# Who adds the expert values of the later rows: TensorE and VectorE by halves, or VectorE alone outside the attentions

## The chip, the cores and the metric

The kernel runs on one core of one Trainium2 chip. The metric is the device time of one execution in microseconds, median over runs. All arithmetic is fp32 (float32r, in high and low parts, for the large weight products).

## The reference, cut to what matters

Two transformer blocks over 512 tokens of width 1024. The first ends in a layer of experts (`peer_ffn`): each token takes 128 experts of 16384 (8 heads, 16 each), and

```python
ue = jnp.take(expert_u, expert, axis=0)          # 128 rows of 1024 per token
ve = jnp.take(expert_v, expert, axis=0)          # 128 rows of 1024 per token
h = jax.nn.gelu(jnp.einsum('thkd,td->thk', ue, xc), approximate=False)
return jnp.einsum('thk,thkd->td', gate * h, ve)
```

The second block is a differential attention, a feed-forward layer (1024 to 4096 to 1024, squared relu), a latent attention and another feed-forward layer.

## The kernel before

**Rows.** The experts are worked off in 512 "rows". Row n belongs to token tile tt = n // 128 (128 tokens, one on each partition) and to the k-th chosen expert, k = n % 128. For a row, GpSimd issues one indirect DMA (line 1708) that brings for each of the 128 tokens 2048 numbers, u and v of its k-th expert, 1 MB in all. VectorE multiplies u by the token's x and sums (`dve_dot`, line 1826, 1024 columns, `accum_out`). ScalarE makes the gelu, the weight gate × gelu, and a diagonal matrix of the weights (`act_weight`, lines 1776, 1778, 1783). Then weight × v is added to the tile's sum in PSUM: up to row 255 TensorE does it alone, two products diag × v of 512 columns (line 1727). From row 256 on TensorE adds columns 0 to 511 into bank 6 and VectorE columns 512 to 1023 into bank 7, as one scalar_tensor_tensor (line 1808, with the weight as a scalar read from SBUF) that reads and writes PSUM. After k = 127 ScalarE copies the sums out (`act_join`, line 1792) and TensorE transposes them back (`pe_join`).

**Buffers.** From row 236 on the rows go round six buffers (`row_of`), so the gather of row n waits until row n - 6 has been added. `late` puts the adding of rows from 256 on one step later than the dot: in step s VectorE does the dot of row s + 1 and then the adding of row s - 1, and TensorE its product of row s - 1.

**What the later rows run beside.** Every engine has its own instruction list, in an order written out by hand. Rows 256 to 511 are interleaved with the second block's first 256 tokens (`tail(self.halves[0])`): `beside` takes one piece of the second block, adds its weight times RATE (1.1) to a due count, and lets as many row steps follow. So all engines have the row steps at the same places between the pieces, and each engine works strictly in order. A piece is one product group of 24 matmuls of 256 columns in the large layers (weight 1), or one block of an attention (weight 1.2; an attention has 16 blocks of scores and 19 such pieces). In the order of time: the join and the q, k and v products (27 pieces' weight), attention (22.8), its output layer with the norm of the heads (10), feed-forward (64), the second attention's projections (19.5), attention (22.8), its output layer (8), feed-forward (64, the rows end before it does). The second 256 tokens follow with no rows beside them.

**Weights of the second block** come in tiles of 512 KB (SyncE's queue, line 283). ScalarE makes the high part (`act_hi`, line 292), GpSimd the low part (`pool_lo`, line 298). GpSimd has both the low parts and the gathers in one list, so a gather that waits for its buffer holds up the low parts behind it. In a feed-forward layer VectorE scales a product (line 2503), ScalarE squares and rounds it (2487, 2491), VectorE makes the low part (2506); VectorE adds the layer's output to the residual (2530). The tail's products use PSUM banks 0 to 3.

Of the kernel before, what the change touches and what calls it, by code (L numbers as in the profile page):

```python
# [187 lines left out]
class Net:  # L188
    def __init__(self, nc, ctx, dram):
# [6 lines left out]
        self.spot, self.turn = {}, 0  # L196
        self.used, self.emptied = {}, {}
# [1210 lines left out]
    @staticmethod  # L1408
    def both_add(n):

        return n >= 256
# [275 lines left out]
    def pool_rows(self, e):  # L1687
        S = "peer_pool"
        lows = [k for k in self.keys if len(k) == 3]
        at = 0  # L1690
        for n in range(512):
            tt, k, r = n // 128, n % 128, self.row_of(n)
            before = self.row_before(n)
            while n >= FEW_ROWS + 12 and at < len(lows) and self.spot_before(lows[at]) <= self.spot.get(("row", before), 0):
                self.pool_lo(e, lows[at])
                at += 1
            if k == 0:
                e.wait_ge(*self.at("peer_dve", ("expert", tt)))
            if before is not None:
                e.wait_ge(*self.at("peer_pe", ("acc", before)))  # L1700
                if self.both_add(before):
                    e.wait_ge(*self.at("peer_dve", ("acc", before)))
            elif r == 0:
                e.wait_ge(*self.at("peer_pe", ("xn", 3, 1)))
            elif r == 6:
                e.wait_ge(*self.at("peer_pe", "mod20"))
            index = bass.IndirectOffsetOnAxis(ap=self.chosen[tt][:, k:k + 1], axis=0)
            e.indirect_dma_start(self.rows[r], None, self.d["peer_uv"], index).then_inc(*self.tick(f"row{r}", n, 16))  # L1708
        for key in lows[at:]:
            self.pool_lo(e, key)  # L1710
# [5 lines left out]
    def pe_rows(self, e):  # L1716
        S, D_, A_ = "peer_pe", "peer_dve", "peer_act"
        for step in range(-1, 512 + LAG):
            n = self.late(step)
            if n is not None:  # L1720
                tt, k = n // 128, n % 128
                b = 4 if tt == 0 else 6
                if k == 0 and tt >= 2:
                    e.wait_ge(*self.at(A_, ("sums", tt - 1)))
                e.wait_ge(*self.at(A_, ("diag", n)))
                for half in range(1 if self.both_add(n) else 2):
                    ins = e.matmul(self.ps[:, b + half, :], self.diag[n % 4],  # L1727
                                   self.rows[self.row_of(n)][:, 1024 + 512 * half:1536 + 512 * half], start=k == 0,
                                   stop=k == 127)
                ins.then_inc(*self.tick(S, ("acc", n)))  # L1730
                self.spot[("row", n)] = self.turn
# [18 lines left out]
    def act_rows(self, e):  # L1750
        S, D_, P_ = "peer_act", "peer_dve", "peer_pe"
        for n in range(-1, 512 + LAG):
# [5 lines left out]
            if n + 1 < 512:  # L1758
                self.act_weight(e, n + 1)
            if self.late(n) in (127, 255, 383, 511):  # L1760
# [6 lines left out]
            yield  # L1767

# [3 lines left out]
    def act_weight(self, e, n):  # L1772
# [7 lines left out]
        if n >= 4:  # L1780
            e.wait_ge(*self.at("peer_pe", ("acc", n - 4)))
# [3 lines left out]

    def act_join(self, e, tt):
        b = 4 if tt == 0 else 6
        e.wait_ge(*self.at("peer_pe", ("acc", 128 * tt + 127)))
# [5 lines left out]
    def dve_rows(self, e):  # L1794
        S, A_, P_ = "peer_dve", "peer_act", "peer_pe"
        for step in range(-1, 512 + LAG):
            if step + 1 < 512:
                self.dve_dot(e, step + 1)
            n = self.late(step)
            if n is not None and self.both_add(n):  # L1800
                v, w, acc = self.rows[self.row_of(n)][:, 1536:2048], self.weight[:, n % 128:n % 128 + 1], self.ps[:, 7, :]
                e.wait_ge(*self.at(A_, ("weight", n)))
                if n % 128 == 0:
# [11 lines left out]
    def dve_dot(self, e, n):  # L1815
# [6 lines left out]
        if self.both_add(n):  # L1822
# [235 lines left out]
    def attention(self, H, scores, softmaxed, turn, meet):  # L2058
        blocks = [(hh, qb) for hh in range(8) for qb in (2 * H.h, 2 * H.h + 1)]
        for n in range(len(blocks) + 3):  # L2060
# [8 lines left out]
            yield 1.2  # L2069

# [973 lines left out]
```

## Time and profile before

| | |
|---|---|
| median of 3 runs | 3439.2 us (3437.33 to 3441.46) |
| the profiled execution: its time | 3435.03 us |
| its span, first to last instruction | 3433.1 us |
| rows 256 to 511 beside the second block's first half | 1425 to 2580 us of the span |
| rows 0 to 255 | 760 to 1425 us |

Busy times are those of one profiled execution. The clock column is the share of TensorE's full speed that was granted (1.00 is 2.4 GHz, 0.50 is 1.2 GHz). The DMA column is the mean busy share of 16 DMA engines. "Idle before" is the time in which the engine stood still ahead of an instruction, with the instruction that let it go on.

### The profile page before, as it was taken

To read this page: it belongs to the slowest core of one execution; us is meant where nothing else is said; L and a number is where in the kernel's file an instruction comes from. 1 tells how busy PE (TensorE), PEld (TensorE's weight loads), DVE (VectorE), ACT (ScalarE), POOL (GpSimd) and SP (SyncE) were. 2 spreads that over 40 slices of the span, in tenths; PEclk is the share of its full clock that TensorE was granted. 3 is DMA by queue.
4 is the path that set the end of the run, shared out by engine and by line. 5 is a ranking of instruction groups with operands and counts; after the bars stand their busy time and mean duration, and the time that the engine had idled before them with its cause. 6 is when DMAs were issued, how large, how long until landed. Compare 5 with 4: busy or idle time off the path is not lost.

```text
span 3433.1 us, 43369 instructions
## 1 busy us (share of the span) xinstructions
PE 2812.6 (82%) x15438; PEld 2166.3 (63%) x15438; DVE 1986.8 (58%) x4260; ACT 1431.1 (42%) x3189; POOL 1659.1 (48%) x1014
## 2 busy tenths in 40 slices
PE   6987987778787777698688888688886979988897
PEld 4847986553333322385467766367776868977897
DVE  5775444457777767676665567675555453244422
ACT  2223222223333433457554445764443444344433
POOL 3812212363444433373276756266763426651674
PEclk8989998889999999797798988899987989999999
DMA  7210001329999998888598888888983314531453
GB/s 279 99 49 1 1 1 49 135 97 422 421 421 421 421 420 348 335 332 319 219 348 334 335 328 320 297 333 332 347 337 135 111 50 150 163 117 55 140 166 100
DMA packets 140518, 797.49 MB, mean 232 GB/s; under 512 B 15504, under 2 KB 18704, under 8 KB 67600
## 3 DMA queue, kind: packets, MB, share of 16 engines
q0 software_dynamic: 73728, 536.90, 38.9%
q1 hardware_dynamic: 65856, 253.36, 21.6%
q10 hardware_dynamic: 720, 4.46, 0.3%
q8 instruction: 124, 2.03, 0.2%
q14 instruction: 90, 0.74, 0.1%
HBM read 788.10 MB, written 6.55 MB: 231 GB/s over the span
## 4 chain that ended last, share of the span: by engine, by line
PE 39%; DMA 16%; POOL 12%; DVE 12%; issue 9%; ACT 6%; ACTq 0%; DVEq 0%; POOLq 0%; SPq 0%
PE ps L1727 7%; DMA raw<-in_peer_uv,un 6%; PE ps L2457 6%; POOL wls L298 6%; PE ps L870 6%; PE ps L1925 6%; DMA w<-in_peer_uv,un 5%; PE ps L328 4%; POOL wlw L298 4%; DMA un<-in_peer_uv,un 3%; PE ps L2435 2%; DVE scratch L1826 2%; POOL raw L1708 1%; DVE ps L1808 1%; PE ps L2122 1%
## 5 line engine op out<-in xcount | busy, mean ns | idle before, releaser
L298 POOL TENSOR_TENSOR wls<-raws,whs 128x1024 fp32r<-128x1024 f32 (+1 forms) x256 | 606.3, 2381 | 398.5 <-ACT whs L292 397.2
L1727 PE MATMUL ps<-raw,un 128*128 128x512 f32 x760 | 405.2, 650 | 134.1 <-ACT un L1783 131.8
L1708 POOL DMA_INDIRECT raw<-in_peer_uv,un x276 | 281.4, 1019 | 374.9 <-PE ps L1727 165.2
L1776 ACT ACTIVATE un<-un 128x1 f32<-128x1 f32 x512 | 103.6, 202 | 684.4 <-DVE scratch L1826 658.5
L292 ACT CAST whs<-raws 128x1024 fp32r<-128x1024 f32 (+1 forms) x256 | 260.8, 1036 | 198.7 <-PE ps L2457 85.4
L298 POOL TENSOR_TENSOR wlw<-raws,whw 128x1024 fp32r<-128x1024 f32 x112 | 265.7, 2389 | 110.8 <-ACT whw L292 110.4
L1727 PEld LDWEIGHTS ps<-raw,un 128*128 128x128 f32 x760 | 137.5, 203 | 278.1 <-ACT un L1783 199.3
L1925 PE MATMUL ps<-ts,whs 128*128 128x256 f32 x1424 | 298.1, 310 | 17.1 <-DVE ts L1994 9.6
L2457 PE MATMUL ps<-ts,whs 128*128 128x256 f32 x1216 | 261.1, 310 | 33.7 <-POOL wlw L298 29.9
L1727 PE MATMUL ps<-w,un 128*128 128x512 f32 x384 | 201.6, 670 | 88.7 <-ACT un L1783 88.7
L1925 PEld LDWEIGHTS ps<-ts,whs 128*128 128x128 f32 x1424 | 240.0, 204 | 46.9 <-issue 33.9
L1727 PE MATMUL ps<-un 128*128 128x512 f32 x392 | 217.3, 667 | 58.2 <-ACT un L1783 58.2
L1826 DVE SCALAR_TENSOR_TENSOR scratch<-raw,ps 128x1024 f32<-128x1024 f32 x172 | 209.0, 1215 | 75.3 <-DMA raw<-in_peer_uv,un 69.8
L1708 POOL DMA_INDIRECT un<-in_peer_uv,un x140 | 137.3, 981 | 214.4 <-DVE ps L1808 110.8
L2457 PEld LDWEIGHTS ps<-ts,whs 128*128 128x128 f32 x1216 | 203.9, 203 | 58.1 <-POOL wlw L298 32.3
L1783 ACT ACTIVATE un<-kept,un 128x128 f32<-128x128 f32 x512 | 205.7, 402 | 48.6 <-ACT un L1778 1.5
L2435 PE MATMUL ps<-ts,whw 128*128 128x256 f32 x960 | 202.7, 312 | 26.0 <-DVE ts L1994 22.9
L2435 PE MATMUL ps<-ts,whs 128*128 128x256 f32 x1088 | 220.5, 304 | 0.0
L1925 PE MATMUL ps<-ts,wls 128*128 128x256 f32 x712 | 208.9, 293 | 0.0
L1727 PEld LDWEIGHTS ps<-w,un 128*128 128x128 f32 x384 | 76.1, 210 | 208.0 <-ACT un L1783 136.6
L298 POOL TENSOR_TENSOR wl<-raw,wh 128x2048 fp32r<-128x2048 f32 x23 | 106.9, 4654 | 202.0 <-ACT wh L292 202.0
L2530 DVE TENSOR_TENSOR kept<-kept,ps 128x256 f32<-128x256 f32 x256 | 103.6, 418 | 164.4 <-PE ps L2457 163.4
(426 smaller groups left out, 7129.9 us busy)
## 6 DMA issues: line engine op xcount, KB each, us to landing
raws<-in_w_up SPq DMA_DIRECT2D x128, 512.0 KB
raws<-in_w_down SPq DMA_DIRECT2D x128, 512.0 KB
raws<-in_w_qk SPq DMA_DIRECT2D x32, 512.0 KB
scratch<-in_ada_w SPq DMA_DIRECT2D x13, 1024.0 KB, 14.4
raw<-in_w_in SPq DMA_DIRECT2D x11, 1024.0 KB, 5.8
raw<-in_ada_w SPq DMA_DIRECT2D x11, 1024.0 KB, 4.8
raw<-in_peer_w_q SPq DMA_DIRECT2D x8, 1024.0 KB, 7.0
raws<-in_w_v SPq DMA_DIRECT2D x16, 512.0 KB
```

What stands on the lines that cost most here:

```text
L292: e.copy(self.wh[h][:, 0:width], self.raw[slot][:, 0:width]).then_inc(*self.tick("hi", key))
L298: e.tensor_tensor(self.wl[h][:, 0:width], self.raw[slot][:, 0:width], self.wh[h][:, 0:width].bitcast(F32), ALU.subtract).then_inc(*self.ti ...
L328: ins = e.matmul(self.ps[:, b, :], l, r, start=k == 0 and i == 0, stop=k == nk - 1 and i == 2)
L870: ins = e.matmul(self.ps[:, b, 128 * q:128 * q + 128], l, r, start=n == 0, stop=n == len(terms) - 1)
L1708: e.indirect_dma_start(self.rows[r], None, self.d["peer_uv"], index).then_inc(*self.tick(f"row{r}", n, 16))
L1727: ins = e.matmul(self.ps[:, b + half, :], self.diag[n % 4], self.rows[self.row_of(n)][:, 1024 + 512 * half:1536 + 512 * half], start=k == ...
L1776: e.activation(self.gelus[:, c], self.dots[:, c], ACT.Gelu, bias=0.0, scale=1.0).then_inc(*self.tick(S))
L1783: e.activation(self.diag[n % 4], self.C("ident"), ACT.Identity, bias=0.0, scale=self.weight[:, c]).then_inc(*self.tick(S, ("diag", n)))
L1826: e.scalar_tensor_tensor(out=self.junk[n % 2 if n < 256 else 1], in0=self.rows[r][:, 0:1024], scalar=1.0, in1=xn, op0=ALU.mult, op1=ALU.mu ...
L1925: ins = e.matmul(o[:, 0:256], l, r, start=k == 0 and i == 0, stop=k == nk - 1 and i == 2)
L2435: ins = e.matmul(o[:, 0:256], l, r, start=k == 0 and n == 0, stop=k == 7 and n == 2)
L2457: ins = e.matmul(o[:, 0:256], l, r, start=n == 0, stop=n == 11)
```

## The change

Rows that are worked while an attention is being issued stay shared, as before. For all other rows from 256 on, VectorE adds all 1024 columns into banks 6 and 7 in one instruction; TensorE has no product and ScalarE makes no diagonal for them. VectorE's adding moves one step ahead for every row from 256 on: in step s it does the dot of row s + 1 and adds row s. TensorE's product of a shared row stays where it was. Where a shared stretch begins inside a token tile, TensorE can't continue VectorE's sum in bank 6, so ScalarE copies the bank to SBUF (`act_carry`) and TensorE starts its sum with ident × copy; where the stretch ends, VectorE waits once for TensorE's last product. A gather waits for TensorE only where row n - 6 was shared, and the copy at a tile's end (`act_join`) waits for VectorE's last row and for the last shared one.

```diff
+        self.shared_rows, self.attending = set(), False
...
-    @staticmethod
-    def both_add(n):
-        return n >= 256
+    def pe_adds(self, n):
+        return n < 256 or n in self.shared_rows
+
+    def pe_row_before(self, n):
+        return max((m for m in range(n - n % 128, n) if self.pe_adds(m)), default=None)
...
             if before is not None:
-                e.wait_ge(*self.at("peer_pe", ("acc", before)))
-                if self.both_add(before):
+                if self.pe_adds(before):
+                    e.wait_ge(*self.at("peer_pe", ("acc", before)))
+                if before >= 256:
                     e.wait_ge(*self.at("peer_dve", ("acc", before)))
...
+            if step >= 256 and self.attending:
+                self.shared_rows.add(step)
+            if n is not None and self.pe_adds(n):
...
+                first, last = k == 0 or not self.pe_adds(n - 1), k == 127 or not self.pe_adds(n + 1)
+                if first and k:
+                    e.wait_ge(*self.at(A_, ("carry", n)))
+                    e.matmul(self.ps[:, b, :], self.C("ident"), self.sums[tt % 2][:, 0:512], start=True, stop=False)
                 e.wait_ge(*self.at(A_, ("diag", n)))
-                for half in range(1 if self.both_add(n) else 2):
+                for half in range(2 if n < 256 else 1):
                     ins = e.matmul(self.ps[:, b + half, :], self.diag[n % 4],
-                                   self.rows[self.row_of(n)][:, 1024 + 512 * half:1536 + 512 * half], start=k == 0,
-                                   stop=k == 127)
+                                   self.rows[self.row_of(n)][:, 1024 + 512 * half:1536 + 512 * half],
+                                   start=first and k == 0, stop=last)
...
+            if n % 128 and self.pe_adds(n) and not self.pe_adds(n - 1):
+                self.act_carry(e, n)
...
-        if n >= 4:
-            e.wait_ge(*self.at("peer_pe", ("acc", n - 4)))
+        if not self.pe_adds(n):
+            return
+        user = max((m for m in range(n % 4, n, 4) if self.pe_adds(m)), default=None)
+        if user is not None:
+            e.wait_ge(*self.at("peer_pe", ("acc", user)))
...
+    def act_carry(self, e, n):
+        tt = n // 128
+        e.wait_ge(*self.at("peer_dve", ("acc", n - 1)))
+        if tt == 3:
+            e.wait_ge(*self.at("peer_pe", ("join", 1, 1)))
+        e.copy(self.sums[tt % 2][:, 0:512], self.ps[:, 6, :]).then_inc(*self.tick("peer_act", ("carry", n)))
...
-            n = self.late(step)
-            if n is not None and self.both_add(n):
-                v, w, acc = self.rows[self.row_of(n)][:, 1536:2048], self.weight[:, n % 128:n % 128 + 1], self.ps[:, 7, :]
+            n = step
+            if 256 <= n < 512:
+                w, row = self.weight[:, n % 128:n % 128 + 1], self.rows[self.row_of(n)]
+                v, acc = (row[:, 1536:2048], self.ps[:, 7, :]) if self.pe_adds(n) else (row[:, 1024:2048], self.sum_banks())
                 e.wait_ge(*self.at(A_, ("weight", n)))
+                pe = self.pe_row_before(n)
+                if pe is not None and not self.pe_adds(n):
+                    e.wait_ge(*self.at(P_, ("acc", pe)))
...
         blocks = [(hh, qb) for hh in range(8) for qb in (2 * H.h, 2 * H.h + 1)]
+        self.attending = True
         for n in range(len(blocks) + 3):
...
+        self.attending = False
```

## Rows read from the trace of the kernel before

**Rows 1.** The page: busy us, share of the span and instructions of each engine

```profile
PE 2812.6 (82%) x15438; PEld 2166.3 (63%) x15438; DVE 1986.8 (58%) x4260; ACT 1431.1 (42%) x3189; POOL 1659.1 (48%) x1014
```

**Rows 2.** Windows: length, busy of PE, PEld, DVE, ACT, POOL, clock, DMA share, GB/s

```profile
1425.00:1560.00 135.00, 114.82 (x707) 94.14 (x707) 93.86 (x198) 72.21 (x168) 84.40 (x52) 0.91 0.85 333
1560.00:1667.00 107.00, 85.75 (x273) 47.29 (x271) 80.38 (x229) 88.17 (x213) 26.29 (x27) 0.76 0.76 282
1667.00:1735.00 68.00, 46.97 (x260) 38.74 (x261) 40.34 (x86) 31.18 (x69) 33.75 (x21) 0.77 0.61 236
1735.00:2052.00 317.00, 270.14 (x1689) 226.69 (x1688) 188.89 (x369) 151.99 (x357) 207.32 (x132) 0.91 0.89 336
2052.00:2162.00 110.00, 83.92 (x424) 62.41 (x423) 84.21 (x158) 63.25 (x140) 65.83 (x44) 0.86 0.87 336
2162.00:2246.00 84.00, 56.72 (x196) 34.88 (x197) 53.89 (x137) 69.78 (x155) 20.00 (x22) 0.84 0.77 273
2246.00:2290.00 44.00, 35.65 (x239) 30.50 (x238) 33.80 (x56) 27.51 (x62) 35.85 (x21) 0.97 0.99 386
2290.00:2580.00 290.00, 249.46 (x1552) 208.68 (x1552) 165.80 (x320) 135.14 (x316) 190.36 (x117) 0.92 0.86 326
```

**Rows 3.** Instruction groups, 1425 to 2580 us: count | busy us, mean ns | idle before

```profile
L1826 DVE SCALAR_TENSOR_TENSOR scratch<-raw,ps 128x1024 f32<-128x1024 f32 x172 | 209.0, 1215 | 75.3 <-DMA raw<-in_peer_uv,un 69.8 <-ACT ps L1757 2.8 <-issue 2.6
L1727 PE MATMUL ps<-raw,un 128*128 128x512 f32 x345 | 201.2, 670 | 86.3 <-ACT un L1783 84.2 <-ACT un L1792 2.1
...
L1808 DVE SCALAR_TENSOR_TENSOR ps<-raw,un,ps 128x512 f32<-128x512 f32 x170 | 127.6, 751 | 0.0
...
L1727 PE MATMUL ps<-un 128*128 128x512 f32 x176 | 108.8, 706 | 28.8 <-ACT un L1783 28.8
...
L1783 ACT ACTIVATE un<-kept,un 128x128 f32<-128x128 f32 x258 | 103.7, 402 | 24.1 <-ACT un L1778 0.4
...
L1826 DVE SCALAR_TENSOR_TENSOR scratch<-un,ps 128x1024 f32<-128x1024 f32 x84 | 102.0, 1215 | 38.5 <-DMA un<-in_peer_uv,un 36.6 <-ACT un L1783 1.9
...
L1808 DVE SCALAR_TENSOR_TENSOR ps<-un,ps 128x512 f32<-128x512 f32 x84 | 63.1, 751 | 0.0
...
L2506 DVE TENSOR_TENSOR ts<-ps,ts 128x256 fp32r<-128x256 f32 x64 | 27.2, 425 | 131.2 <-ACT ts L2491 130.3 <-ACT ps L2487 0.8
...
L1994 DVE SCALAR_TENSOR_TENSOR ts<-kept,ts 128x256 fp32r<-128x256 f32 x32 | 15.5, 485 | 0.3 <-ACT ts L1966 0.3
```

**Rows 4.** The windows view of line 1727 alone, first feed-forward stretch

```profile
1735.00:2052.00 317.00, 81.65 (x142) 23.39 (x142) 0.91 0.89 336
```

**Rows 5.** Waits, 1735 to 2052 us: who waited for whom, us in total, times, longest

```profile
DVE ts L2506 <- ACT ts L2491: 65.5, 31, 5.6
POOL raw L1708 <- DVE ps L1808: 42.8, 20, 3.8
...
PE ps L1727 <- ACT un L1783: 35.8, 14, 7.5
POOL un L1708 <- DVE ps L1808: 24.4, 9, 5.6
DVE scratch L1826 <- DMA raw<-in_peer_uv,un: 20.1, 16, 2.7
...
DVE scratch L1826 <- DMA un<-in_peer_uv,un: 17.5, 12, 3.5
...
DVE ps L2503 <- PE ps L2435: 9.6, 10, 2.4
```

**Rows 6.** Timeline of VectorE: start, us, instruction, idle before it

```profile
1811.83 0.42 DVE L2506 TENSOR_TENSOR ts<-ps,ts 128x256 fp32r<-128x256 f32 x1 [0.84 <-ACT ts L2491]
```

**Rows 7.** Windows: TensorE after an idle gap; the second half without rows

```profile
1804.30:1809.10 4.80, 4.78 (x16) 3.75 (x17) 2.23 (x4) 3.25 (x9) 3.68 (x2) 0.50 0.76 239
...
2900.00:3000.00 100.00, 92.27 (x726) 91.57 (x726) 24.82 (x61) 42.55 (x64) 75.50 (x32) 0.95 0.53 163
```

**Rows 8.** Instruction groups of the whole run: a ScalarE copy of 512 columns

```profile
L1601 ACT COPY scratch<-ps 128x512 f32<-128x512 f32 x16 | 9.3, 587 | 39.2 <-PE ps L1573 21.6 <-DVE scratch L1675 15.5 <-PE ps L1727 2.0
```

More of the change, by code:

```diff
@@ L1719, in pe_rows @@
             n = self.late(step)
-            if n is not None:
+            if step >= 256 and self.attending:
+                self.shared_rows.add(step)
+            if n is not None and self.pe_adds(n):
                 tt, k = n // 128, n % 128
@@ L1724, in pe_rows @@
                     e.wait_ge(*self.at(A_, ("sums", tt - 1)))
+                first, last = k == 0 or not self.pe_adds(n - 1), k == 127 or not self.pe_adds(n + 1)
+                if first and k:
+                    e.wait_ge(*self.at(A_, ("carry", n)))
+                    e.matmul(self.ps[:, b, :], self.C("ident"), self.sums[tt % 2][:, 0:512], start=True, stop=False)
                 e.wait_ge(*self.at(A_, ("diag", n)))
-                for half in range(1 if self.both_add(n) else 2):
+                for half in range(2 if n < 256 else 1):
                     ins = e.matmul(self.ps[:, b + half, :], self.diag[n % 4],
-                                   self.rows[self.row_of(n)][:, 1024 + 512 * half:1536 + 512 * half], start=k == 0,
-                                   stop=k == 127)
+                                   self.rows[self.row_of(n)][:, 1024 + 512 * half:1536 + 512 * half],
+                                   start=first and k == 0, stop=last)
                 ins.then_inc(*self.tick(S, ("acc", n)))
+            if n is not None:
                 self.spot[("row", n)] = self.turn
@@ L1767, in act_rows, with sum_banks @@
             yield
+    def sum_banks(self):
+        return self.ps[:, 6:8, :].rearrange("p b n -> p (b n)")
     def xn_bank(self):
@@ L1784, in act_weight @@
                      scale=self.weight[:, c]).then_inc(*self.tick(S, ("diag", n)))
+    def act_carry(self, e, n):
[4 more added lines that the diff above has]
+        e.copy(self.sums[tt % 2][:, 0:512], self.ps[:, 6, :]).then_inc(*self.tick("peer_act", ("carry", n)))
     def act_join(self, e, tt):
         b = 4 if tt == 0 else 6
-        e.wait_ge(*self.at("peer_pe", ("acc", 128 * tt + 127)))
+        last = self.pe_row_before(128 * tt + 127) if tt >= 2 and not self.pe_adds(128 * tt + 127) else 128 * tt + 127
+        if last is not None:
+            e.wait_ge(*self.at("peer_pe", ("acc", last)))
         if tt >= 2:
@@ L1821, in dve_dot @@
         xn = self.XN[:, n // 128, :]
-        if self.both_add(n):
+        if n >= 256:
             e.wait_ge(*self.at("peer_act", ("xn", n // 128)))
```

## The prediction

> **What bounds the kernel now.** I read the page first: TensorE is busy 82% of the span and VectorE 58% [rows 1]. That average hides stages with different limits, so the next view is the windows of the stage that the change touches, 1425 to 2580 us, cut where the second block goes from one layer to the next [rows 2]. In it VectorE is busy 741 of 1155 us. In the two feed-forward stretches (317 and 290 us) TensorE is busy 85 and 86%, and the DMA engines 89 and 86%, since every row brings 1 MB and every piece of the second block a 512 KB weight tile.
>
> For one piece of weight 1 in a feed-forward layer, the first has 64 pieces in 317 us: 4.95 us per piece, with 1.1 rows in it. What does each engine need?
> - TensorE: in the second half, without rows, 726 matmuls take 100 us, so 24 take 3.31 us [rows 7]. The row products take 81.65 us for 71 rows, 1.15 us a row [rows 4]. Together 3.31 + 1.1 × 1.15 = 4.57 us, 92% of 4.95.
> - DMA: 0.89 × 4.95 = 4.41 us.
> - VectorE: 188.9 / 64 = 2.95 us, and half a wait of 0.84 us, the shortest that it has between lines 2503 and 2506 while ScalarE squares and rounds [rows 6]: 3.37 us.
>
> So two limits stand close together, TensorE just above DMA, and the in-order lists lose the rest. The waits of that stretch show how [rows 5]: TensorE stands 35.8 us for a row's diagonal, GpSimd 42.8 + 24.4 us for VectorE to have added the row whose buffer the next gather wants, and VectorE 65.5 us for ScalarE but only 9.6 us for TensorE's product.
>
> **The change part by part.** Each attention has pieces worth 22.8, so 22.8 × 1.1 = 25 rows; two attentions make 50 shared rows, and 206 of the 256 move.
> - *TensorE's products go*: 206 × 1.15 = 237 us of TensorE, out of the busiest engine. A feed-forward piece then needs 3.31 us of it. ScalarE loses 206 diagonals of 402 ns [rows 3], 83 us, and their wait for TensorE's product of row n - 4.
> - *VectorE's adding grows* from 512 to 1024 columns. No row shows this shape. A scalar_tensor_tensor with a scalar from memory takes 485 ns for 256 columns (line 1994) and 751 for 512 (line 1808), 266 ns for 256 columns more; so 751 + 532 = 1283 ns. The lower bound is the 1024-column dot that reads PSUM, 1215 ns (+464); the upper one is two of the old addings, 1502 (+751) [rows 3]. I take +532, as its rows are of the same kind: 206 × 0.532 = 110 us (96 to 155). A piece then needs 3.37 + 1.1 × 0.532 = 3.96 us of VectorE. Nothing hides this on VectorE itself, which works in order; it is covered only where VectorE would otherwise stand idle, 414 us in this stage, of which 106 us are waits for rows' data [rows 3].
> - *The adding moves a step ahead.* It now waits for the weight of a row whose dot was finished one dot earlier; the dot in between takes 1.2 us and ScalarE's gelu and weight are short, so I cost this at nothing. That cover is gone where ScalarE is stuck behind a weight tile that has not landed. Behind a waiting adding stand the next piece's scaling or residual, and TensorE waits for those. On the other side the buffer comes free one step (some 4.5 us) sooner: row n was added after the dot of row n + 2 and is now added after that of n + 1. Before, three rows beyond the one in work could be in flight, now four. GpSimd's 67 us of waits are what this shortens. Its list issues the same gathers and low parts in the same order.
> - *A gather no longer waits for TensorE* outside the attentions; TensorE can run ahead of the rows by its four free banks, so the 35.8 us go from it. In the attentions a gather waits for TensorE's product, which is still a step late, so little changes there.
> - *Two carries*: a copy of 512 columns, nearest 587 ns [rows 8], and one product more, 1.15 us, twice: 3.5 us if nothing covers it. The wait at the end of a shared stretch comes once each and I cost it at nothing, as TensorE's product is due in the same step; if TensorE lags, it is one piece.
>
> DMA's bytes stay. A feed-forward piece after the change needs 4.41 us of DMA, 3.96 of VectorE, 3.31 of TensorE. The floor moves from 4.57 to 4.41 only: that is why 237 us of TensorE's work can't come back as 237 us. How close the stretch comes to its floor is a choice: it is at 92% of its tightest engine now, and one stretch (2246 to 2290) shows DMA at 0.99 [rows 2]. I take a DMA share of 0.93, and let VectorE be busy at most 85% (the rows show up to 77%; the waits for ScalarE inside a piece leave no more):
> - 1425 to 1560: DMA 135 × 0.85 / 0.93 = 123; VectorE (93.9 + 24 × 0.532) / 0.85 = 125.5. New length 125.5, **-9.5**.
> - 1735 to 2052: 317 × 0.89 / 0.93 = 303, **-14** (VectorE 226.7, 75%).
> - 2290 to 2580: 290 × 0.86 / 0.93 = 268, **-22** (VectorE 165.8 + 66 × 0.532 = 200.9, 75%).
> - 2052 to 2162: VectorE (84.2 + 25 × 0.532) / 0.85 = 115; there the chain through norms and small pieces sets the time. **0**.
> - 2246 to 2290: DMA is full; VectorE (33.8 + 11 × 0.532) / 0.85 = 46.6, **+2.6**.
> - 1667 to 1735, where the norm of the heads leaves every engine waiting: **0**. The attentions: 0, with the carries **+3.5**.
>
> The sum is -39 us. From the profiled execution's 3435.0 us (its span of 3433.1 and 1.9 around it) that is 3396; that execution is 4.2 us under the median of the runs, so against the median it is 3439.2 - 39 = **3400 us**.
>
> **The clock.** TensorE's granted clock was 0.50 (1.2 GHz) from 1804.3 to 1809.1, after 7.5 us of waiting for a diagonal, and 0.91 over the first feed-forward stretch [rows 2, 5, 7]. The Trainium skill, "TensorE: Matmul & The Clock Gate" (HAM oscillation), says that an engine whose short bursts are parted by waits for data starts each burst cold; it speaks against making TensorE idler. By rows, a piece all at half clock would take 3.31 × 0.95 / 0.5 = 6.3 us instead of 4.95, +1.34 × 124 pieces = +166 us, 3605 us. TensorE decides only below a mean clock of 3.31 × 0.95 / 4.7 = 0.67, and the idlest stretches show 0.76 and 0.77 [rows 2]. By that rule, this case so far agrees only in part, and I give it 0.02.
>
> **The rivals.**
> - *The forecast*, 3375 to 3425: both feed-forward stretches move toward DMA's floor. Chance 0.45.
> - *DMA gets full* because a fourth row in flight keeps it fed: the stretches of 135, 317, 290 and 110 us shrink by their free DMA share (0.15, 0.11, 0.14, 0.13), 20 + 35 + 41 + 14 = 110 us, 3329 us. For it: GpSimd's 67 us of waits for buffers [rows 5]. Against it: VectorE would be at 80 to 100% in them. 3325 to 3375, chance 0.18.
> - *VectorE takes the place of TensorE and it comes out even*: in the first feed-forward stretch VectorE has 317 - 189 = 128 us idle. If only its waits for rows, 20.1 + 17.5, go, and those for ScalarE stay, the new length is 226.7 + 90.5 = 317 us. For it: VectorE hardly waits for TensorE. Against it: ScalarE is late partly because its diagonals wait for TensorE. Within 7 us of 3439: 0.14. Between this and the forecast, 3425 to 3432: 0.06.
> - *Slower*: VectorE's adding, now bound to the weight of the step before, waits for a ScalarE that stands behind a weight tile, so that VectorE keeps half of its row waits too. The 110 us are then paid and 53 come back: +57, 3496 us; it decides from where VectorE wins back less than 110 of its 414 idle us. For it: VectorE's largest wait is already for ScalarE. Chance 0.15.
> - If the change moved fewer rows than 206 (more of them counted as inside an attention), all terms shrink alike; the count of the new shape will tell. It gets no chance of its own.
>
> **How the numbers follow.** The time is the likeliest case's, 3400 us, its own range 3375 to 3425. The range for 8 in 10 leaves out the slow cases (0.17) and the bottom of the full DMA: 3335 to 3444. About 0.2%, 7 us, is what a measurement can tell from no change. Faster: 0.45 + 0.18 + 0.06 = 0.69; same 0.14; slower 0.15 + 0.02 = 0.17.
>
> **What the changed profile would show.** Right: some 206 instructions of VectorE with 1024 columns into PSUM at about 1.28 us, two copies by the carry; TensorE's busy time down by some 240 us; in the feed-forward stretches a DMA share of 0.93 or more, VectorE at 75%, GpSimd's waits for VectorE well under 67 us, and VectorE waiting more for ScalarE or DMA than for anything else. Wrong: a DMA share that stays at 0.89 with VectorE over 80% (the even case), VectorE waiting for the weight at its adding (the slower one), or a granted clock under 0.7. A price near 1.5 us for the new adding would cost 45 us of VectorE more and lead to the even case.

## The result, and the profile after

| | before | after |
|---|---|---|
| median | 3438.3 us (3435.5 to 3441.5, 4 runs) | 3465.8 us (3459.7 to 3468.9, 4 runs) |
| ratio, 95% interval | | 1.0083 [1.0070, 1.0096] |
| the profiled execution: its time / span | 3435.0 / 3433.1 us | 3465.0 / 3463.2 us |
| mean granted clock | 0.903 | 0.879 |

The change made the kernel 27.5 us slower, where 39 us faster was forecast. The page after, as in [rows 1]:

```profile
PE 2679.2 (77%) x15030; PEld 2139.4 (62%) x15030; DVE 2114.7 (61%) x4260; ACT 1348.8 (39%) x2985; POOL 1660.9 (48%) x1014
```

TensorE has 408 matmuls fewer in the records. Each product of a row is there as two, so these are 412 for 206 rows, less four for the two carries. Its busy time fell by only 133 us. VectorE gained 128 us with the same number of instructions.

The windows view, cut at the same events of the second block as [rows 2] (the first cut is at 1428 us, where both kernels are still level):

```profile
1428.00:1581.00 153.00, 98.50 (x641) 91.76 (x640) 130.68 (x190) 55.71 (x129) 75.03 (x48) 0.83 0.71 271
...
1750.00:2080.00 330.00, 230.07 (x1556) 221.84 (x1555) 229.97 (x376) 131.09 (x298) 219.69 (x138) 0.82 0.88 336
...
2312.00:2610.00 298.00, 207.24 (x1433) 200.25 (x1433) 206.44 (x333) 115.11 (x263) 197.91 (x122) 0.85 0.86 331
```

The same first stretch of the kernel before:

```profile
1428.00:1558.00 130.00, 110.54 (x694) 92.28 (x694) 91.18 (x193) 69.44 (x159) 81.86 (x50) 0.91 0.84 330
```

It took 130 us with VectorE busy for 91.18 of them. Now it takes 153, and VectorE is busy 130.68 us in it with three instructions fewer. That is 22 to 23 us lost in the stretch that the forecast had get 9.5 us shorter. The 17 + 8 larger addings of that stretch add 13 us to VectorE; something else adds 26, net. In the feed-forward stretches the DMA share did not rise (0.88 and 0.86, before 0.89 and 0.86), and they are 12 and 9 us longer over their whole lengths (318 to 330, 317 to 326). By the time of the second feed-forward layer's end the kernel after is 32 us behind; the remainder of the program takes 834 us in it and 836 in the kernel before.

The groups view of 1428 to 2629 us for the lines that answer to [rows 3]:

```profile
L1861 DVE SCALAR_TENSOR_TENSOR scratch<-raw,ps 128x1024 f32<-128x1024 f32 x172 | 208.8, 1214 | 54.4 <-DMA raw<-in_peer_uv,un 52.3 <-ACT ps L1770 2.1
L1843 DVE SCALAR_TENSOR_TENSOR ps<-raw,un,ps 128x1024 f32<-128x1024 f32 x137 | 175.9, 1284 | 7.3 <-ACT un L1796 7.3
...
L1843 DVE SCALAR_TENSOR_TENSOR ps<-un,ps 128x1024 f32<-128x1024 f32 x67 | 86.0, 1284 | 0.0
...
L2543 DVE TENSOR_TENSOR ts<-ps,ts 128x256 fp32r<-128x256 f32 x64 | 27.2, 425 | 101.7 <-ACT ts L2528 101.7
...
L1843 DVE SCALAR_TENSOR_TENSOR ps<-raw,un,ps 128x512 f32<-128x512 f32 x33 | 24.8, 752 | 2.3 <-ACT un L1796 2.3
...
L2179 DVE TENSOR_TENSOR q<-q,tmp 128x256 f32<-128x256 f32 x8 | 18.8, 2346 | 0.3
L2179 DVE TENSOR_TENSOR k<-k,tmp 128x256 f32<-128x256 f32 x8 | 18.7, 2342 | 0.3
```

The new adding is there 204 times, with two first rows of a tile in another form, 206 in all, at 1284 ns; the shared rows are 33 + 17 = 50. All waits of VectorE for the weight at its adding together are 7.3 + 2.3 + 1.1 us. The last two rows are the find. Line 2179 is the last instruction of the rotary step, `x = x + tmp` on 256 columns; it belongs to the second block, and the change does not touch it. In the kernel before, the same sixteen instructions, in the same view of 1428 to 1560 us:

```profile
L2142 DVE TENSOR_TENSOR k<-k,tmp 128x256 f32<-128x256 f32 x8 | 3.4, 426 | 0.3
L2142 DVE TENSOR_TENSOR q<-q,tmp 128x256 f32<-128x256 f32 x8 | 3.4, 425 | 0.3
```

37.5 us instead of 6.8: 31 us of VectorE. (Of its other instructions, the dots above all, some 4 us less fall into the window, hence the 26 net.) Fourteen of the sixteen take 2.57 to 2.64 us; the first and the last take 0.42. The timelines of VectorE and then GpSimd in the kernel after (start, us, instruction, idle before it) show what the instruction does in that time:

```profile
1504.78 1.28 DVE L1843 SCALAR_TENSOR_TENSOR ps<-un,ps 128x1024 f32<-128x1024 f32 x1
1505.98 0.41 DVE L2176 TENSOR_TENSOR tmp<-ps,rsin 128x256 f32<-128x256 f32 x1
1506.31 0.41 DVE L2177 TENSOR_TENSOR q<-q,rc 128x256 f32<-128x256 f32 x1
1506.76 2.63 DVE L2179 TENSOR_TENSOR q<-q,tmp 128x256 f32<-128x256 f32 x1
1509.31 1.21 DVE L1861 SCALAR_TENSOR_TENSOR scratch<-raw,ps 128x1024 f32<-128x1024 f32 x1
...
1510.45 1.28 DVE L1843 SCALAR_TENSOR_TENSOR ps<-un,ps 128x1024 f32<-128x1024 f32 x1
```

```profile
1506.71 2.40 POOL L299 TENSOR_TENSOR wls<-raws,whs 128x1024 fp32r<-128x1024 f32 x1 [1.77 <-ACT whs L293]
1509.25 0.96 POOL L1714 DMA_INDIRECT un<-in_peer_uv,un  x1
```

The sum starts 0.05 us after GpSimd's low part of a weight tile (line 299) and ends 0.28 us after it, at 1509.39. The profile books this as busy time, so no view of waits names it. The kernel before, VectorE and GpSimd:

```profile
1501.59 0.42 DVE L2139 TENSOR_TENSOR tmp<-ps,rsin 128x256 f32<-128x256 f32 x1 [1.14 <-PE ps L2134]
1501.93 0.42 DVE L2140 TENSOR_TENSOR k<-k,rc 128x256 f32<-128x256 f32 x1
1502.38 0.43 DVE L2142 TENSOR_TENSOR k<-k,tmp 128x256 f32<-128x256 f32 x1
1502.72 1.21 DVE L1826 SCALAR_TENSOR_TENSOR scratch<-raw,ps 128x1024 f32<-128x1024 f32 x1
```

```profile
1502.55 2.52 POOL L298 TENSOR_TENSOR wls<-raws,whs 128x1024 fp32r<-128x1024 f32 x1 [0.38 <-ACT whs L292]
```

Here the sum starts 0.17 us ahead of the low part and is done in 0.43 us; it is the low part that takes 2.52 us for 2.40. What sets the order is visible in the chains. After the change both instructions hang on the same event, the end of a dot (1504.86). On VectorE the adding (1.28 us) and two rotary instructions follow it; on ScalarE gelu, weight, a copy and the high part do, and the low part waits for that. Both chains take 1.85 to 1.9 us, so the two meet again in the next period, 5.67 us later. Before, VectorE's adding was 0.53 us shorter, its period was 4.17 us, and the two engines met only after a wait of 1.14 us for TensorE's product and with another phase. That the longer adding shifts the sums into the low parts is read from these chains; x2 and x3 below test it.

The Trainium skill, "SBUF — State Buffer" (the section "SBUF: two separate sides"), has the rule for it: VectorE and GpSimd share one pair of ports as an exclusive lock, and an instruction of VectorE with two inputs in SBUF waits for all of a GpSimd instruction that reads SBUF if that one started first. The rows above agree: `q` and `tmp` both lie in SBUF, the low part reads two tiles of SBUF, the sum that started 0.05 us after it was held and the one that started 0.17 us ahead of it was not, and the addings, whose second large input is the bank, keep their 1284 ns. Closer than 0.1 us the recorded starts do not follow the rule: see x14.

### The profile page after: what moved, and what is told of

Same layout as the page of the kernel before. It is cut to its first block, busy times and chain, and to the rows that moved or that the text cites. A ratio compares the mean times of both kernels' runs of the same rounds, so it can differ in the third digit from the quotient of the medians.

```text
span 3463.2 us, 41943 instructions
## 1 busy us (share of the span) xinstructions
PE 2679.2 (77%) x15030; PEld 2139.4 (62%) x15030; DVE 2114.7 (61%) x4260; ACT 1348.8 (39%) x2985; POOL 1660.9 (48%) x1014
## 4 chain that ended last, share of the span: by engine, by line
PE 35%; DMA 17%; DVE 17%; POOL 11%; issue 8%; ACT 7%; DVEq 0%; ACTq 0%; POOLq 0%; SPq 0%
DMA raw<-in_peer_uv,un 6%; PE ps L2494 6%; POOL wls L299 6%; PE ps L871 6%; DMA w<-in_peer_uv,un 5%; PE ps L1739 5%; PE ps L329 4%; PE ps L1960 4%; DVE scratch L1861 4%; POOL wlw L299 3%; DVE ps L1843 3%; DMA un<-in_peer_uv,un 3%; PE ps L2472 2%; DMA raws<-in_w_down 1%; ACT whs L293 1%
## 5 line engine op out<-in xcount | busy, mean ns | idle before, releaser
L2494 PE MATMUL ps<-ts,whs 128*128 128x256 f32 x1216 | 269.7, 318 | 123.9 <-POOL wlw L299 66.9
L1960 PE MATMUL ps<-ts,whs 128*128 128x256 f32 x1424 | 294.4, 308 | 24.5 <-DVE ts L2029 14.1
L2494 PEld LDWEIGHTS ps<-ts,whs 128*128 128x128 f32 x1216 | 222.1, 224 | 132.0 <-POOL wlw L299 71.8
L1739 PE MATMUL ps<-raw,un 128*128 128x512 f32 x482 | 250.9, 656 | 55.1 <-ACT un L1804 55.1
L1960 PEld LDWEIGHTS ps<-ts,whs 128*128 128x128 f32 x1424 | 246.3, 210 | 32.9 <-issue 16.2
L1861 DVE SCALAR_TENSOR_TENSOR scratch<-raw,ps 128x1024 f32<-128x1024 f32 x172 | 208.8, 1214 | 54.4 <-DMA raw<-in_peer_uv,un 52.3
L2494 PE MATMUL ps<-ts,whw 128*128 128x256 f32 x832 | 183.3, 314 | 71.9 <-POOL wls L299 33.2
L2472 PE MATMUL ps<-ts,whw 128*128 128x256 f32 x960 | 193.7, 303 | 47.6 <-DVE ts L2029 41.0
L1739 PEld LDWEIGHTS ps<-raw,un 128*128 128x128 f32 x482 | 92.8, 207 | 188.4 <-ACT un L1804 107.8
L1843 DVE SCALAR_TENSOR_TENSOR ps<-raw,un,ps 128x1024 f32<-128x1024 f32 (+1 forms) x170 | 200.7, 1180 | 9.6 <-ACT un L1796 9.6
L2472 PE MATMUL ps<-ts,whs 128*128 128x256 f32 x1088 | 197.8, 284 | 4.6 <-DVE kept L2567 3.2
```

What stands on the lines that cost most here:

```text
L1739: ins = e.matmul(self.ps[:, b + half, :], self.diag[n % 4], self.rows[self.row_of(n)][:, 1024 + 512 * half:1536 + 512 * half], start=first ...
L1843: e.scalar_tensor_tensor(out=acc, in0=v, scalar=w, in1=acc, op0=ALU.mult, op1=ALU.add).then_inc(*self.tick(S, ("acc", n)))
L1861: e.scalar_tensor_tensor(out=self.junk[n % 2 if n < 256 else 1], in0=self.rows[r][:, 0:1024], scalar=1.0, in1=xn, op0=ALU.mult, op1=ALU.mu ...
L1960: ins = e.matmul(o[:, 0:256], l, r, start=k == 0 and i == 0, stop=k == nk - 1 and i == 2)
L2472: ins = e.matmul(o[:, 0:256], l, r, start=k == 0 and n == 0, stop=k == 7 and n == 2)
L2494: ins = e.matmul(o[:, 0:256], l, r, start=n == 0, stop=n == 11)
```

## Experiments

Three theories stood at the start. *Held*: the rotary sums, held by GpSimd's instructions, cost the 28 us. *Larger adding*: VectorE's 110 us more cost it by themselves, held sums or not. *Step ahead*: the adding's earlier place costs it. The expectations call them theories A, B and C. Two more came later, on what sets the pace of the feed-forward layers: D, the transfers, and E, VectorE's in-order list. The medians of the kernel before in the three groups of runs are 3436.7, 3436.0 and 3435.5 us; each ratio is to the kernel before in its own group, so differences of medians across groups carry up to 3 us of drift. The ratios are not the quotients of the medians either: for x1 the two differ by 3 us.

**x1_rope_psum**: the kernel after, with the rotary product left in its PSUM bank, so that the sum has only one input in SBUF. The bank is thus given back only after the sum.

```diff
-        e.tensor_tensor(tmp, self.bh((P_, "rope", key)), rsin, ALU.mult)...
+        r = self.bh((P_, "rope", key))
+        e.tensor_tensor(r, r, rsin, ALU.mult)...
...
-        e.tensor_tensor(x, x, tmp, ALU.add)...
+        e.tensor_tensor(x, x, r, ALU.add)...
```

> The changed kernel, but the rotary sum of a q or k tile (x = x + tmp) reads its product from PSUM, where the product was made in place, so that this instruction of VectorE has one operand in SBUF instead of two. Theory A (VectorE's instruction with two SBUF operands, 2345 ns instead of 426, is held by GpSimd's low part that starts just before it; 31 us in the q/k products): the instruction goes back to 0.43 us, the stretch up to the first scores falls from 152 to 125-133 us, the kernel from 3466 to 3440-3448. Theory B (the longer adding of 1024 columns on VectorE's in-order list is the whole cost): the instruction's time is an effect and something else takes its place, 3460-3470. Theory C (the adding a step ahead is the cost): also 3460-3470.

Measured: 3433.5 us (3422.5 to 3436.2, 10 runs), 0.9982 [0.9968, 0.9995]. The sum in the groups view of 1428 to 1553 us:

```profile
L2180 DVE TENSOR_TENSOR q<-q,ps 128x256 f32<-128x256 f32 x8 | 3.4, 421 | 0.3
```

The first attention's scores begin at 1552.6 us instead of 1580.6. The change of one operand's place takes back 32 us, all of the slowdown and more than the 18 to 26 us expected.

**x8_before_rope_psum**: the same edit in the kernel before.

> The kernel before, with the rotary sum read from PSUM. Before the change the sum was not held (426 ns), so if the gain of the changed kernel by this edit comes from the held instruction alone, this gains nothing: within 7 us of before. If reading PSUM helps in another way (32 us in the changed kernel), 3405-3425.

Measured: 3437.6 us (10 runs), 1.0007 [0.9994, 1.0020]. The edit is worth nothing where the sums are not held, so its 32 us in x1 are the price of the holding.

**x12_rope_sum_later**: the kernel after, both operands in SBUF, with the sum issued one piece later.

```diff
         e.tensor_tensor(x, x, rc, ALU.mult)...
+        if key in range(15) and S.startswith("diff"):
+            self.rope_left = (x, tmp, S, key)      # rope_sum() issues it before the next rotary step
+            return
```

> The changed kernel with the rotary sum as it was, both operands in SBUF, but of the first attention's q and k tiles it is issued one piece later, ahead of the next tile's rotary work and behind a row's dot and adding. Theory A (held only while GpSimd's low part runs): it starts when the low part is over or before it begins, takes 0.43 us in most cases, and the kernel comes to 3430-3450. If the form with two SBUF operands were slow by itself here, it stays at 2.3 us and the kernel at 3466.

Measured: 3466.0 us (4 runs), 1.0099 [1.0076, 1.0123]. The expected time was missed, for a reason that the groups and the timelines of VectorE and GpSimd show:

```profile
L2178 DVE TENSOR_TENSOR q<-q,rc 128x256 f32<-128x256 f32 x8 | 18.2, 2278 | 0.0
...
L2190 DVE TENSOR_TENSOR q<-q,tmp 128x256 f32<-128x256 f32 x8 | 3.3, 412 | 0.0
```

```profile
1505.38 2.52 DVE L2178 TENSOR_TENSOR q<-q,rc 128x256 f32<-128x256 f32 x1
```

```profile
1505.25 2.37 POOL L300 TENSOR_TENSOR wls<-raws,whs 128x1024 fp32r<-128x1024 f32 x1 [1.77 <-ACT whs L294]
```

The sum is free at 0.41 us, and `x * rc`, the next instruction with two inputs in SBUF, is held in its place for 2.3 us. It starts 0.13 us after the low part. So the holding is not bound to one instruction but to the place in the period, and moving this one did not help.

**x14_split_low**: the kernel after, with GpSimd's low part for the q and k weights in four instructions of 256 columns.

```diff
+        cut = 4 if key[0] == "w_qk" and len(key) == 3 else 1
+        for i in range(cut):
+            c = slice(width * i // cut, width * (i + 1) // cut)
...
```

> The changed kernel, the rotary work untouched, but GpSimd makes the low part of a w_qk tile in four instructions of 256 columns instead of one of 1024. If VectorE's instruction with two SBUF operands is held until GpSimd's running instruction is over, it now waits for a quarter: the sum falls from 2.35 to 0.8-1.2 us, and the kernel to 3440-3450. If GpSimd keeps the memory for as long as it has work, the sum stays at 2.3 us or longer and the kernel at 3466 or above.

Measured: 3451.3 us (3442.6 to 3455.4, 10 runs), 1.0038 [1.0025, 1.0052], half of the loss back, just outside the 3440 to 3450 expected. VectorE's timeline, then GpSimd's:

```profile
1504.74 0.96 DVE L2182 TENSOR_TENSOR q<-q,tmp 128x256 f32<-128x256 f32 x1
...
1508.73 3.17 DVE L2182 TENSOR_TENSOR q<-q,tmp 128x256 f32<-128x256 f32 x1
```

```profile
1504.69 2.99 POOL L302 TENSOR_TENSOR wls<-raws,whs 128x256 fp32r<-128x256 f32 x4 [0.98 <-ACT whs L293]
...
1508.80 2.81 POOL L302 TENSOR_TENSOR wls<-raws,whs 128x256 fp32r<-128x256 f32 x4
```

Where the sum starts 0.04 to 0.05 us after the first part, it gets in behind that part (0.96 us, six of the sixteen). Where it starts 0.07 to 0.10 us ahead of it, it waits for all four (3.17 to 3.21 us, four of them), longer than before the cut. One was free, and the last five (2.51 to 2.76 us) met the v weights' low parts, which the edit leaves whole. So the cut helps by the place where the two meet, and not throughout. That the hold shrinks with GpSimd's instruction in six sums shows that it is this instruction that holds them. But four sums were held though they started ahead by the records, and through four instructions; a fifth, 0.07 us ahead of an uncut low part, was held as well (2.76 us). By the recorded starts that is not the rule cited above.

**x2_half_left_out**: the kernel after, with columns 0 to 511 of the moved rows left out, so that VectorE's adding is as long as before.

```diff
-  ... if self.pe_adds(n) else (row[:, 1024:2048], self.sum_banks())
+  ... if self.pe_adds(n) or n % 128 else (row[:, 1024:2048], self.sum_banks())
```

> The changed kernel, but VectorE's adding stays at columns 512 to 1023 in all moved rows except the first of a token tile: columns 0 to 511 of the moved rows are added by nobody (left out of the computation). TensorE's and ScalarE's work is gone as in the change, VectorE's is as before. Theory B: the removal itself gains, the growth of VectorE loses more; feed-forward stretches of 318 and 300 us fall to 290-305 and 270-285, the kernel 3385-3415. Theory A predicts that the gain is spoilt in the q/k products if the instruction with two SBUF operands is still held (3405-3430). If taking work from TensorE gains nothing, since TensorE then runs at a lower clock or DMA sets the pace anyway: 3430-3445. Theory C: near 3450 or above.

Measured: 3412.9 us (4 runs), 0.9927 [0.9902, 0.9952]. By itself this run can't tell the two theories apart, because with the shorter adding the sums (424 ns) were no longer held either. It does show that the holding needs the longer adding.

**x13_rope_psum_half_left_out**: x1 and x2 together, with the same columns left out.

> The changed kernel with the rotary sum from PSUM, and VectorE's adding kept at 512 columns in all moved rows but the first of a tile: columns 0 to 511 of the moved rows are left out of the computation. Against the same with all columns (3434) it prices VectorE's 110 us more by themselves: if they are covered by waits for rows and weight tiles (theory D), 3415-3434; if VectorE's list sets the pace (theory E), 3370-3400.

Measured: 3409.8 us (5 runs), 0.9926 [0.9902, 0.9950]. That is in neither of the two ranges expected. Between x1 and x13 lie only VectorE's 110 us: by the medians 3433.5 - 3409.8 = 24 us, by the two ratios 19, with some 9 us of uncertainty, so about a fifth of them. Between the kernel before and x13 lie TensorE's products gone (237 us by the forecast's price), ScalarE's diagonals and the waits for TensorE gone with them, and the step ahead, all together: 26 us. They do not lie where the forecast had them: x13's feed-forward layers take 317 and 318 us, as in the kernel before (318 and 317). It gains 9 us up to the first scores, 7 from there to the first feed-forward layer and 10 between the two layers.

**x5_before_ahead**: the kernel before, with VectorE's adding a step ahead and nothing else.

```diff
-            n = self.late(step)
-            if n is not None and self.both_add(n):
+            n = step
+            if n < 512 and self.both_add(n):
```

> The kernel before, with one part of the change alone: VectorE adds its 512 columns a step ahead (in step s the dot of row s + 1, then the adding of row s). TensorE still has its product of every row, one step late. If the earlier step is what frees buffers, GpSimd still waits for TensorE's product here: within 7 us of before. If it costs (the adding waits for the weight), 3445-3460. If it moves VectorE against GpSimd so that the rotary sum is held, the sum's duration will show it.

Measured: 3429.0 us (10 runs), 0.9986 [0.9973, 1.0000]: a gain of some 5 to 7 us, at the edge of what can be told from nothing. The step ahead by itself does not cost, and the sums stay free (425 ns).

**x3_step_late**: the kernel after, with the adding put back a step.

```diff
-            n = step
-            if 256 <= n < 512:
+            n = self.late(step)
+            if n is not None and 256 <= n < 512:
```

> The changed kernel, but VectorE adds a row one step late again, as before (in step s the dot of row s + 1 and the adding of row s - 1). Theory B with my prediction's account of the buffers: one row less in flight, GpSimd waits longer for VectorE, and the kernel gets slower than the change, 3475-3495. Theory C (the adding now waits for a ScalarE that stands behind a weight tile): faster, 3440-3455. Theory A says nothing of the step, but if the phase between VectorE and GpSimd shifts, the held instruction may come free, which its duration will show.

Measured: 3465.1 us with its four runs far apart (3451.3, 3453.0, 3477.2, 3489.4), 1.0104 [1.0049, 1.0160]; the median is in neither of the ranges expected. In the profiled one (3453.0) the sums took 425 ns, and the second feed-forward layer 338 us, against 324 in x1. So the late step has a cost of its own in this kernel, and frees the sums: they are held only with the adding both longer and a step ahead; what scatters its runs by 38 us was not found.

**x4_ff_only**: rows are moved in the feed-forward layers alone and stay shared elsewhere.

```diff
+        self.attending = False
         yield from self.pe_mlp(e, H, 0)
+        self.attending = True
```

> The changed kernel, but rows count as shared in all layers except the two feed-forward ones: about 136 rows move instead of 206. Theory A: the q/k stretch goes back to 130 us, and what is left is the feed-forward layers' own loss: 3445-3457. Theory B alone in proportion to the rows moved (136 of 206 of +27 us): 3457. If the feed-forward layers alone lose nothing, 3439.

Measured: 3433.3 us (3427.1 to 3439.7, 10 runs), 0.9990 [0.9979, 1.0000]. The sums are free (426 ns); the first scores begin at 1565.2 us, 7 us later than in the kernel before, with the rows shared there as in it. The two feed-forward layers take 314 us each, before 318 and 317. The change, put only where the forecast had seen its gain, gives there at most 4 + 3 us and not 14 + 22. Even these can't be told from nothing: in the profiled execution of x8, which changes nothing in these layers, the second takes 311 us. And the same instructions as in x4 take 323 and 324 us in x1, which has moved rows outside the layers too and reaches the first one 19 us earlier. Why was not found; a layer's length alone is a weak measure, and x1 and x4 are the same as wholes (3433.5 and 3433.3 us).

**x9_half_gathers** and **x15_before_half_gathers**: x1 and the kernel before, with gathers from row 256 on that bring 1024 numbers of each expert and not 2048 (the other half of the buffer keeps old numbers; all instructions stay).

```diff
+  dst, src = self.rows[r][:, 0:1024], self.d["peer_uv"].rearrange("r (t c) -> (r t) c", t=2)
```

> The changed kernel with the rotary sum read from PSUM, but the gathers of rows 256 to 511 bring 1024 numbers per token instead of 2048 (row i of the table seen as 32768 rows of 1024; the values are what the buffers held, so this data is not computed on): half of the rows' bytes, all instructions kept. Theory D (in the feed-forward stretches DMA's transfers set the pace, at a share near 0.89 that nothing raises): both stretches fall from 323 and 324 us to 280-300 and the kernel to 3360-3400. Theory E (VectorE's in-order list sets it there): 315-325 each, the kernel 3420-3435.

> The kernel before, with the gathers of rows 256 to 511 bringing 1024 numbers per token instead of 2048 (row i of the table seen as 32768 rows of 1024; the values are what the buffers held). If TensorE was the limit in the feed-forward layers before (4.57 of 4.95 us per piece), halving the rows' bytes gains much less than the 55 us that it gained in the changed kernel: 3410-3435. If transfers were the limit already, the same 45-60 us: 3376-3391.

Measured: x9 3378.5 us (4 runs), 0.9843 [0.9825, 0.9861], 55 us under x1. x15 3372.4 us (4 runs), 0.9809 [0.9777, 0.9841], 63 us under the kernel before, a little more than expected. The first feed-forward layer in the windows view of x1, x13, x9 and x15:

```profile
1723.00:2046.00 323.00, 224.03 (x1553) 216.22 (x1552) 228.90 (x375) 130.40 (x298) 219.91 (x138) 0.85 0.89 342
```

```profile
1717.00:2034.00 317.00, 220.34 (x1558) 212.57 (x1557) 195.21 (x376) 130.62 (x298) 219.87 (x138) 0.85 0.90 350
```

```profile
1718.00:2020.00 302.00, 219.08 (x1551) 212.65 (x1550) 229.23 (x376) 128.23 (x292) 218.88 (x138) 0.87 0.68 238
```

```profile
1733.00:2023.00 290.00, 257.85 (x1692) 217.08 (x1691) 188.06 (x368) 151.84 (x355) 208.42 (x131) 0.97 0.72 237
```

The last row is the telling one. With all of TensorE's products in it, the layer of the kernel before runs in 290 us, 4.53 us a piece, once half of the gathers' bytes are gone. So TensorE's work did not hold it at 317. (Its granted clock was 0.97 here and 0.91 before; its busy time went from 270 to 258 us.)

**x10_rope_psum_defer**: x1, with VectorE's low part (the instruction that waits longest for ScalarE) issued a piece later in the feed-forward layers.

```diff
-            e.wait_ge(*self.at(A_, ("hi", g, t)))
-            e.tensor_tensor(lo, x, hi.bitcast(F32), ALU.subtract)...
+            left.append((g, t, lo, x, hi))      # issued ahead of the next piece's scaling
```

> The changed kernel with the rotary sum from PSUM, and in the feed-forward layers VectorE makes a tile's low part (line 2543) at the start of the next piece, behind the row's dot and adding, instead of standing idle while ScalarE squares and rounds. Theory E: VectorE wins back some 50 us of waits per feed-forward layer, and the kernel falls from 3433 to 3395-3415. Theory D: the waits turn into waits for rows, 3425-3435.

Measured: 3438.3 us (10 runs), 1.0002 [0.9989, 1.0015]. No gain. The waits view of its first feed-forward layer:

```profile
PE ps L2496 <- DVE ts L2552: 39.4, 10, 8.1
...
DVE scratch L1861 <- DMA raw<-in_peer_uv,un: 32.2, 17, 6.7
...
DVE ps L1843 <- ACT un L1796: 25.1, 6, 6.4
```

VectorE's wait for ScalarE became TensorE's wait for VectorE and VectorE's wait for rows' data; the layer takes 328 us, against 323 in x1 (the profiled execution, 3451.1 us, is the slowest of the ten).

## Why the prediction was wrong, by its own steps

The account, from the runs by their medians: TensorE's products gone and the step ahead -26 (x13), VectorE's 110 us +24 (x1 less x13), the held sums +32 (the kernel after less x1). By the ratios the three are -25, +19 and +35. The terms are differences along one chain of runs, so that they add up to the measured +28 (but for the drift between the groups) tests nothing; the split is what they tell.

Against the forecast's -39 three steps failed: it had no term for held instructions (+32), it hid all of VectorE's growth outside two short stretches (+24), and it credited the feed-forward layers with 36 us that no version with whole gathers got there (x13's 26 us lie in other stretches).

- *The count and the price* were right: 206 rows, 50 shared, 1284 ns for 1283, so the 266 ns per 256 columns went on up to 1024 columns in two banks. ScalarE lost 82 us of busy time for the 83 named. The carries' copies took 1.1 us in all, but TensorE waited 15.7 us for the two; no run prices that.
- *The first stretch, -9.5*: the step that failed most. The sum had VectorE's time there as its old busy time plus 24 × 0.532 and no term for an instruction of VectorE that grows because of when it starts. The stretch came out 22 to 23 us longer. The larger adding's own price was right; its length, with its earlier place, shifted what follows it into GpSimd's low part (x2, x3). The trace of before had the thing itself, in the second attention's rotary step, on VectorE and on GpSimd:

```profile
2146.68 2.59 DVE L2140 TENSOR_TENSOR qr<-qr,mrc 128x256 f32<-128x256 f32 x1
```

```profile
2146.62 2.35 POOL L298 TENSOR_TENSOR wls<-raws,whs 128x1024 fp32r<-128x1024 f32 x1
```

The instruction starts 0.06 us after the low part and takes 2.59 us, where the next one of its kind takes 0.42. In the first stretch the same line with `q` has a mean of 480 ns beside 428 with `k`. The minimum and maximum of such groups would have given this rival; of those on record none had it.

- *TensorE just above DMA at 4.57 us a piece*: wrong. The 3.31 us came from the second half [rows 7], 138 ns a matmul with TensorE's idle 8% in it, while DMA's 4.41 is busy time alone. In the stretch itself the other 1547 matmuls took 270.14 - 81.65 = 188.5 us [rows 2, 4], 122 ns each, 2.92 us for 24 of them and 4.2 us a piece with the rows, under DMA's 4.41. x15, with pieces of 4.53 us, is already under the 4.57 that the forecast gave as TensorE's need. So taking TensorE's work away moved no floor in these layers.
- *A DMA share of 0.93*: in the first feed-forward layer it stayed at 0.87 to 0.90 in every version with full gathers (before, after, x1, x2, x4, x5, x10, x13), and with half of the gathers' bytes the layer fell by 21 and 27 us. The transfers' bytes count, as the forecast had it for the changed kernel, but the margin that I took, from 0.89 to 0.93, was a choice, and it is not there. The forecast's -14 and -22 were measured as -4 and -3 (x4), which is within what two executions differ by, and as -1 and +1 where VectorE's part is left out too (x13).
- *VectorE's growth hidden*: mostly right, all but some 24 of the 110 us (19 by the ratios). For these the sum had only some 5 us in two short stretches.
- *The step ahead at nothing*: right in sign, a gain of 5 to 7 us (x5). GpSimd's waits for VectorE's adding fell from 154.7 + 110.8 us to 122.3 + 58.4 over the stage, as named, and little came of it.
- *The rivals*: the slower one named VectorE's wait for the weight. It came out slower, but not so: that wait is 10.7 us in all. The even case is what the kernel does without the holding: x1 is 3 us faster than before by the medians and 6 by the ratio. Its mechanism, that only waits for rows would go and those for ScalarE stay, was right in half: VectorE's waits for ScalarE at its low part fell from 130.3 to 101.7 us, those for rows from 69.8 + 36.6 to 52.3 + 28.8. DMA did not get full.
- *The clock*: it fell to 0.82 to 0.85 in the feed-forward stretches, as its rival said, and no cost of it shows: x13 runs its layer in 317 us at 0.85, with TensorE busy 220 of them, and the kernel before in 318 at 0.91. As x13 also has less work for TensorE, this prices the two together; no run sets the clock alone.
- *TensorE's busy time down by some 240 us*: it fell by 133. In the first feed-forward layer 81.65 us of row products went, and the others grew from 188.5 us (1547 of them) to 230.07 (1556) at the lower clock.

What stays open: why the feed-forward layers settle at a DMA share near 0.89 when one stretch of 44 us shows 0.99 [rows 2]. Fewer bytes shorten them by 21 and 27 us; all row products off TensorE, 34 us less of VectorE (x13, 317 us for 323) and a deferred wait change little. No run separated the transfers' own pace from the time at which their buffers come free, and half gathers change both. Why x1 takes 9 us more than x4 in the same layer is open too. And the runs of x3 scatter for no cause that was found.

x1, the best complete version of the change, is 3 us under the kernel before (6 by the ratio); x4 is 3 us under it; x5, the old sharing with the adding a step ahead, is 7 us under it (5 by the ratio). Between these three nothing can be told.

## What to carry to other kernels

When an instruction of VectorE gets longer, look not only at its own price but at what it pushes against GpSimd: list the instructions of VectorE with two inputs in SBUF, find the phase of GpSimd's long instructions to them, and keep one operand in PSUM where that is free. Before crediting work taken off an engine, work out its need per piece from the stretch's own rows, not from another stage's, and if a second limit stands within a few per cent, test which one gives by taking bytes or work away.

## What was not expected of the hardware

- An instruction of 256 columns took 2342 ns in the mean instead of 425, in fourteen of sixteen cases because it started 0.05 us after a GpSimd instruction of 2.4 us, and the trace shows this as busy time, with no wait.
- The two engines lock in phase: fourteen of sixteen sums met the low part 0.04 to 0.05 us after its start, most of them in one period after another of 5.67 us, and when the sum was moved away (x12), the neighbour took its place.
- By the records the order of the two starts does not always tell who waits: with the cut low part (x14), a sum that started 0.07 to 0.10 us ahead of it was held for 3.2 us, and one 0.04 to 0.05 us behind it for 0.96.
- The same instructions of the first feed-forward layer took 314 us in x4 and 323 in x1, whose rows differ only outside it; no cause was found.
